# Feed-forward rounds with seven block products in place of eight, hidden tiles through memory, and the down product by thirds of the tokens

## What is computed

```python
h = _rmsnorm(x, lw["norm_ffn_w"]) * (1 + sc_f) + sh_f
ffn = (jax.nn.silu(h @ lw["ffn_w1"]) * (h @ lw["ffn_w3"])) @ lw["ffn_w2"]
x = x + g_f * ffn
```

## Time and profile before

| what | value |
| --- | --- |
| runs | 3107.42 us median of 3 (3106.93 to 3108.69) |
| span of the profiled execution | 3106.5 us |
| PE busy | 3060.1 us, 99% |
| PEld busy | 2941.0 us, 95% |
| DVE busy | 1539.3 us, 50% |
| ACT busy | 1217.6 us, 39% |
| POOL busy | 752.6 us, 24% |
| HBM | 210.90 MB read, 36.47 MB written |

### The profile page before, as it was taken

One profiled execution on the slowest core, in us unless ns is written; L12 is line 12 of the kernel. 1 busy time (PEld: TensorE's weight loads), 2 busy tenths in 40 slices (PEclk: granted clock), 3 DMA queues, 4 the chain that ended last, 5 costly groups with the idle time before them and its releaser, 6 DMA issues. The chain is left out here.

```text
span 3106.5 us, 59758 instructions
## 1 busy us (share of the span) xinstructions
PE 3060.1 (99%) x22180; PEld 2941.0 (95%) x22180; DVE 1539.3 (50%) x2647; ACT 1217.6 (39%) x2315; POOL 752.6 (24%) x936
## 2 busy tenths in 40 slices
PE   6999999999999999999999999999999999999998
PEld 5899999999999999999999999999999999999998
DVE  4646657568466574674656333444343222222233
ACT  6445455564554555545545442112241101210222
POOL 0024345245353462353534500000200000000002
PEclk9999999999999999999999999999999999999999
DMA  7622122122231221222212244434111111111112
GB/s 264 246 82 90 41 80 81 48 77 80 65 97 40 82 78 48 86 72 68 86 48 76 91 151 142 136 97 135 39 41 41 41 47 41 47 35 47 41 34 88
DMA packets 291362, 250.61 MB, mean 81 GB/s; under 512 B 10952, under 2 KB 262960, under 8 KB 291120
## 3 DMA queue, kind: packets, MB, share of 16 engines
q1 hardware_dynamic: 255552, 193.40, 20.3%
q10 hardware_dynamic: 35568, 54.02, 5.4%
HBM read 210.90 MB, written 36.47 MB: 80 GB/s over the span
## 5 line engine op out<-in xcount | busy, mean ns | idle before, releaser
L823 PE MATMUL bank<-h_hi,w_hi 128*128 128x384 f32 x2496 | 868.5, 348 | 2.5 <-ACT th L1416 2.5
L823 PE MATMUL bank<-h_hi,w_lo 128*128 128x384 f32 x2496 | 836.6, 335 | 0.0
L823 PE MATMUL bank<-h_lo,w_hi 128*128 128x384 f32 x2496 | 835.8, 335 | 0.0
L2147 PE MATMUL bank<-a_hi,v_hi 128*128 128x384 f32 x1440 | 483.1, 336 | 7.0 <-DVE v_lo L2367 2.5
L823 PEld LDWEIGHTS bank<-h_hi,w_hi 128*128 128x128 f32 x2496 | 469.4, 188 | 17.6 <-issue 7.3
L2147 PE MATMUL bank<-a_hi,v_lo 128*128 128x384 f32 x1440 | 481.1, 334 | 0.0
L2147 PE MATMUL bank<-a_lo,v_hi 128*128 128x384 f32 x1440 | 481.1, 334 | 0.0
L823 PEld LDWEIGHTS bank<-h_lo,w_hi 128*128 128x128 f32 x2496 | 469.8, 188 | 2.7
L823 PEld LDWEIGHTS bank<-h_hi,w_lo 128*128 128x128 f32 x2496 | 469.0, 188 | 0.0
L1935 POOL TENSOR_TENSOR kq<-kq,fg 128x384 f32<-128x384 f32 x288 | 290.0, 1036 | 176.3 <-PE bank L952 145.0
L2147 PE MATMUL bank<-b_hi,v_hi 128*128 128x384 f32 x912 | 306.3, 336 | 0.9 <-DVE v_lo L2367 0.9
(11 more groups left out here) (278 smaller groups left out, 4376.5 us busy)
## 6 DMA issues: line engine op xcount, KB each, us to landing
raw<-in_w_in SPq DMA_DIRECT2D x104, 512.0 KB, 4.1
cumb<-cum_scratch SPq DMA_DIRECT2D x72, 512.0 KB, 6.0
raw<-in_ffn_w SPq DMA_DIRECT2D x60, 512.0 KB, 3.8
ada_late<-in_ada_w SPq DMA_DIRECT2D x8, 2048.0 KB, 9.4
small<-gate_scratch ACTq DMA_DIRECT2D x72, 192.0 KB, 2.4
gate_scratch<-th ACTq DMA_DIRECT2D x48, 192.0 KB, 1.9
y_scratch<-x_t SPq DMA_DIRECT2D x8, 1152.0 KB, 4.8
small<-y_scratch ACTq DMA_DIRECT2D x48, 192.0 KB, 2.4
```

Source lines behind the costliest of these rows:

```text
L823: last = pe.matmul(out, w[i][:, k, :], h[:, k, blk(hb)], start=(k == 0 and j == 0), stop=(k == KT - 1 and j == 2))
L2147: last = pe.matmul(banks[3 * s + b][:, 0:BW], wp[s][:, k, :], operand[ap][:, k, blk(b)], start=(k == 0 and j == 0), stop=(k == kt - 1 and ...
```

## The change

One plain up round of the old kind makes hidden tile 0. The other 21 rounds are made by `pair`. There the two weight blocks of a round are seen as a 2 x 2 block matrix: x11, x12 are the low and high four k-tiles of w1 (`raw[0]`), x21, x22 those of w3 (`raw[1]`). The activations are 2 x 2 as well: low and high four k-tiles, first and second half of the tokens (576 each): a11, a12, a21, a22. Seven products of blocks and some sums give the four blocks of the result:

- sums of weights, in each round, on GpSimd (`s_sums_of`, L3089 to L3098): S1 = x21 + x22, S2 = S1 - x11, S3 = x11 - x21, S4 = x12 - S2. S1 and S3 share a buffer, S2 and S4 the other.
- sums of activations, once, on VectorE and GpSimd (`t_sum_of`, `t_fourth`, L3113), each 4 x 576 columns, split afterwards: T1 = a12 - a11, T2 = a22 - T1, T3 = a22 - a12, T4 = a21 - T2 (over a12).
- products o = 0 to 6: x11 a11, S2 T2, S1 T1, S3 T3, x12 a21, S4 a22, x22 T4, each as two parts j of 288 tokens with 4 k-tiles x 3 terms. Products 4, 5 and 6 add into the banks of 0, 2 and 3.
- sums of results: ScalarE copies product 0 away (`keep_p1`, L2504) before product 4 may add to its bank; VectorE adds U2 (L2837), C22 (L2843, L2845) before products 5 and 6 may add to their banks, C12 (L2855), C21 (L2865), and gates (L2850, L2860); ScalarE does the tanh (L2509, L2514); GpSimd multiplies (`hid_product`, L3107).

Each hidden tile (576 KB) is stored by SP to `hid_scratch`. The weights of the round after are loaded when all seven splits of the running round are made. The core of the diff:

```diff
+BLOCKS = 7
+STEPS = 2 * BLOCKS
+K_BLOCKS = (0, 4, 8, 12, 16, HID)
...
+            with sp.Fori(0, ROUNDS - 1) as rd:
+                sp.wait_ge(x_split, rd * BLOCKS + BLOCKS)
+                load_pair(rd + 1)
+                store_hid(rd)
...
+                        elif o == 4:
+                            pe.wait_ge(p1_kept, rd * 2 + (j + 1))
+                        elif o in (5, 6):
+                            pe.wait_ge(c22_done, rd * 2 + (j + 1))
+                        out = bank_of(o, j)[:, 0:SUB]
+                        for k, (hi, lo) in enumerate(moving(o, j)):
+                            for i, (wi, mv) in enumerate(((0, hi), (0, lo), (1, hi))):
+                                last = pe.matmul(out, w[wi][:, k, :], mv, start=(o < 4 and k == 0 and i == 0),
+                                                 stop=(k == KH - 1 and i == 2),
+                                                 skip_group_check=o >= 4)
+                        last.then_inc(prod_done, 1)
...
+            def pair(rd):
+                for j in range(2):
+                    keep_p1(rd, j, isinstance(rd, int) and rd == 0)
+                for o in range(4):
+                    x_high_part(rd + 1, o)
+                for j in range(2):
+                    tanh1(rd, j)
+                x_high_part(rd + 1, 4)
+                tanh2(rd, 0)
+                x_high_part(rd + 1, 5)
+                tanh2(rd, 1)
+                x_high_part(rd + 1, 6)
...
+                elif which == 3:
+                    pool.wait_ge(x_split, rd * BLOCKS + 3)
+                    pool.tensor_tensor(s0, x11, x21, ALU.subtract).then_inc(s_ready, 1)
```

```diff
+                hid_high_part(h)
...
+                act.activation(hid_hi[b][:, k, :], hid_in[h % 3], ACT.Copy).then_inc(hid_high, 1)
+                load_hid(h + 2)
...
+            def last_pair(rd):
+                for j in range(2):
+                    keep_p1(rd, j)
+                load_hid(0)
+                load_hid(1)
+                for h in range(8):
+                    hid_high_part(h)
+                tanh1(rd, 0)
+                d_high_part(0, 0)
...
+                    for k in range(K_BLOCKS[q], K_BLOCKS[q + 1]):
+                        if t == 0:
+                            pe.wait_ge(hid_split, HID * b + k + 1)
```

More of the change, by code:

```diff
@@ new lines, in down @@
+            def down(u):
+                b, t = divmod(u, OUTS)
+                if u >= 2:
+                    pe.wait_ge(d_added, u - 1)
+                else:
+                    pe.wait_ge(gate1_done, 2 * (ROUNDS - 1) + u + 1)
+                out = banks[u % 2][:, 0:BW]
+                for q in range(QS):
+                    pe.wait_ge(x_split, ROUNDS * BLOCKS + QS * u + q + 1)
+                    w = d_ring(q)
+                    for k in range(K_BLOCKS[q], K_BLOCKS[q + 1]):
+                        if t == 0:
+                            pe.wait_ge(hid_split, HID * b + k + 1)
+                        for i, (wi, mv) in enumerate(((0, hid_hi[b]), (0, hid_lo[b]), (1, hid_hi[b]))):
+                            last = pe.matmul(out, w[wi][:, k - K_BLOCKS[q], :], mv[:, k, :],
+                                             start=(k == 0 and i == 0), stop=(k == HID - 1 and i == 2))
+                    last.then_inc(d_multiplied, 1)
@@ L2203, in _ @@
                 elif name == "up0":
[L2204 to L2213 removed]
+                    for i in range(n):
+                        for s, b in TURNED:
+                            unit(name, i, s, b)
+                            if i == 0 and (s, b) == (0, 0):
+                                ones_product(2)
                 else:
@@ L2216, in _ @@
                         body(name, i)
+            pair(0, True)
+            with pe.Fori(1, ROUNDS) as rd:
+                pair(rd)
+            for u in range(NB * OUTS):
+                down(u)
+                b, t = divmod(u, OUTS)
+                if b > 0 and t == 0:
+                    add_squares(b - 1)
+                elif b > 0 and t == 1:
+                    turn_back(CB * b - 3)
+                    turn_back(CB * b - 2)
+                elif b > 0 and t == 2:
+                    turn_back(CB * b - 1)
+            turn_back(6)
+            turn_back(7)
+            add_squares(2)
+            turn_back(8)
         @block.scalar
@@ L2297, in body, with down @@
+            def down(u):
+                b, t = divmod(u, OUTS)
+                if u > 0:
+                    square_out(u - 1)
+                if b > 0 and t == 1:
+                    root(b - 1)
+                coming = hid_coming(b, t)
+                for q in range(QS):
+                    d_high_part(u + 1, q)
+                    if q < len(coming):
+                        hid_high_part(coming[q])
+            def body(name, i):
                 I = it(name, i)
@@ L2310, in body @@
                             act.dma_start(stage[b][:, :], dram_blk(y_dram, t + y0, b)).then_inc(small_in[b], 16)
-                        if b == 0 and not last_it and not (turned(name, i) and s == 0):
-                            high(s + 1, I, UNITS + 5 if turned(name, i) else None)
+                        if b == 0:
+                            high(s + 1, I)
                         if name in ("s1", "s2"):
@@ L2549, in _ @@
             pool.wait_ge(acc_done, acc_at("h", 3, 1, 2))
+            for late in cleared:
+                pool.sem_clear(late)
             for b in range(NB):
@@ L2580, in _, with s_sums_of @@
-            for b in range(NB):
-                add_square(KT - 2, b, (KT - 2) * NB + 2 * b)
+            def s_sums_of(rd, which):
+                x11, x12, x21, x22 = (raw[i][:, ks, :] for i in range(2) for ks in (slice(0, KH), slice(KH, KT)))
+                s0, s1 = (v[:, :].rearrange("p (k c) -> p k c", c=P) for v in s_sums)
+                if which == 1:
+                    for s in range(2):
+                        pool.wait_ge(x_raw[s], rd * 16 + 16)
+                    pool.tensor_tensor(s0, x21, x22, ALU.add).then_inc(s_ready, 1)
+                elif which == 2:
+                    pool.wait_ge(s_ready, rd * 4 + 1)
+                    pool.tensor_tensor(s1, s0, x11, ALU.subtract).then_inc(s_ready, 1)
+                elif which == 3:
+                    pool.wait_ge(x_split, rd * BLOCKS + 3)
+                    pool.tensor_tensor(s0, x11, x21, ALU.subtract).then_inc(s_ready, 1)
+                else:
+                    pool.wait_ge(s_ready, rd * 4 + 2)
+                    pool.tensor_tensor(s1, x12, s1, ALU.subtract).then_inc(s_ready, 1)
@@ new lines, in _ @@
+            pool.wait_ge(hi_done, PARTS["up"] + 24)
+            pool.wait_ge(parts, PARTS["up"] + 24)
+            second = slice(HALF, T)
+            pool.tensor_tensor(t_sum[:, T2], a_hi[:, KH:KT, second].bitcast(F32), a_lo[:, KH:KT, second].bitcast(F32),
+                               ALU.add).then_inc(h_summed, 1)
+            for which in (1, 2, 3, 4):
+                s_sums_of(0, which)
+            with pool.Fori(0, ROUNDS - 1) as rd:
+                for which in (1, 2, 3, 4):
+                    s_sums_of(rd + 1, which)
+                for j in (2, 3, 0, 1):
+                    hid_product(rd, j)
```

740 lines of the change are left out of this document (555 added, 185 removed).

## The result

| | before | after |
|---|---|---|
| median of the runs | 3108.06 us (3106.93 to 3110.67) | 3140.25 us (3136.76 to 3142.1) |
| ratio | | 1.0101, 95% interval 1.0087 to 1.0116 |
| span of the profiled execution | 3106.5 us | 3140.3 us |

The change makes the kernel 32 us slower, 1.0%; the forecast was 3133. So two measurements of one kernel can lie 4 to 5 us apart, and smaller differences between kernels are read here from their profiles and not from their times.

A forecast was written before the change was run, and what follows sets the result against it. TensorE, busy 99% of the span, was taken to bound the kernel before, a side chain the gated rounds after. Terms: -23 + 31.5 + 0.9 + 17 = +26 us, so 3107.4 + 26 = 3133 us, range 3098 to 3160.

The forecast's parts named there:

- Matmuls of 288 columns: Gated rounds on TensorE: 133 ns a matmul, 168 in 22.4 us, 2.5 us less in each of 21 rounds.
- the rival with 144 ns: Gated rounds: the weight load sets the pace, 24.2 us a round, 10 us more, 3143 us; chance 0.06.
- Side chain: Gated round: store, loads, sums, splits, gates and products take 23.7 us; TensorE needs 22.4 and waits 1.3 us a round.
- the ports' rival: Gated rounds: GpSimd and VectorE slow each other, chain about 1 us longer, 19 us more, 3152 us; chance 0.22.
- 23 us gained: Rounds 2 to 20: 19 x 23.7 = 450 us against 19 x 24.9 = 473.
- First gated round: Four TensorE waits, together 34 us on top of 22.4: 56.4 us against 24.9, 31.5 lost.
- GpSimd's 4.9 us sum hides under VectorE's first three: First gated round: GpSimd's activation sum of 4.9 us adds no time beside VectorE's three sums.
- The clock in that round: First gated round: lowered TensorE clock after gaps mostly falls into waits set by other engines; nothing added.
- Start of down: Down part's start: 14 hidden blocks ready, eight come at 1.3 us or wait for the last store; about 17 us waiting.
- Tail: Transposes, squares and stores at the end keep their length; the one new wait lies beside VectorE's work.
- the one with quicker transfers: Gated rounds: store and loads overlap, chain falls to 22.4 us, TensorE sets the round, 25 us less, 3108; chance 0.15.
- the faster one: Chain of 21.8 us, 130 ns a matmul, hidden blocks in 0.9 us each, down loses 6: 3086 us; chance 0.12.

The follow-up runs named there:

- the second time: The changed kernel with nothing further changed, timed again beside the follow-up runs: 3135.59 us (ratio 1.0089).
- the kernel with loads first: Changed kernel with SP issuing the weight loads of the round after next ahead of the gated blocks' store, not behind it: 3108.31 us.
- twice-stored: Changed kernel with one more store of 576 KB in front of each gated store: 3172.67 us (1.021).
- four kernels: Kernel combining four edits and a reordered first gated round, 3079.67 us; three variants reordering transfers at the start of down: 3079.27, 3077.56, 3076.62 us.

## Why the prediction was right, and where it was off

The sign, the mechanism and most of the size were right: +32 us measured and +28 the second time, +26 forecast, inside the range. Of the first profile's 33.8 us, 4.6 lie before the change, so 29 are the change's. Step by step:

- **Matmuls of 288 columns**: 133 ns forecast, 132 measured (200 us of the kernel with loads first). The load beside them sets nothing; the rival with 144 ns falls.
- **Side chain**: 23.7 us forecast, 23.75 measured, and the loads-first and twice-stored runs show it as the cause: 22.26 us without the store in front (there TensorE sets the round), 25.44 with two. Its terms, from the chain and the timelines of one round: store and loads 7.3 us (2619.92 to 2627.25), as forecast; GpSimd's two sums 2.7 (3.0). Two low parts beside GpSimd's sum and products took 1.03 and 1.24 us for 0.69, so the ports' rival was at work too, with 0.9 us a round, and about as much had been put too high elsewhere. It is no separate case: its price is in the 23.75.
- **"23 us gained" in rounds 2 to 20**, and 0.9 lost in the last: 22.1 together, 20.8 measured over the 20 rounds. The waits are 1.3 x 19 = 25 us as forecast and 25.8 as measured; that the sums agree so well is in part luck, since the 25.8 are 18 waits of 1.3 us in rounds 3 to 20 and one of 2.5 in the last.
- **First gated round**: 31.5 lost was forecast, 38.1 measured. This is the step that was off. "GpSimd's 4.9 us sum hides under VectorE's first three" is wrong: they take turns, the first product started 10.7 us late and not 6; with that sum on VectorE it is 6.3. The delay runs down VectorE's queue. Counted from the end of the plain round, the first, second, fifth and sixth products (each behind one of the four gaps) started at 10.7, 21.7, 41.8 and 55.2 us; the forecast's own steps give 6, 17, 35.6 and 49.3. So 4.7 us are there from the first product on. The further 1.5 us at the fifth are of the same kind: GpSimd's other two sums lie beside VectorE's low parts, of which one took 1.79 us for 0.69, and GpSimd's took 3.55 and 3.64. The last 1.5 us are the halved clock behind the last gap (48 matmuls in 7.8 us, 6.3 at full clock). So the round is 5.9 us late at the sixth product and 7.3 at its end; the forecast's sum stands 0.7 above its own steps, which leaves 6.6.
- **The clock in that round**: "here that mostly falls into waits that are set by the other engines, so I add nothing" was nearly right. In four stretches of 3.2, 6.0, 5.8 and 3.1 us, each behind one of the gaps, TensorE works at a granted clock of 0.5, its lower level of 1.2 GHz, where a matmul takes 0.24 us. Of the 63.0 us, 32.3 are gaps (10.8, 6.4, 8.0 and 7.7 from start to start, less a matmul each), 22.3 are matmuls at full clock, and 8.4 are left for the slower matmuls. But all but 1.5 of these 8.4 us took nothing from the time, since they only shortened the next gap: the chain of that round has no TensorE in it. It also shows from run to run: in four profiles of the same start (the changed kernel twice, the one with the hidden blocks on SP, the one with one more store) the four gaps sum to 33.0 to 34.1 us, while the sixth product starts 55.1 to 55.4 us behind the last plain matmul each time. The 1.5 us at the end were not priced, and round 2, which has no wait, takes most of them back: from the end of the first round's last wait to that of round 3 it is 47.9 us, two rounds of 23.95. No run changed the clock alone. That the four gaps together came out near the forecast's 34 is luck: the forecast had them at full clock and from an earlier start.
- **Start of down**: 17 us forecast, 13.0 measured. Right in kind, but eight blocks at 1.3 us are 10.4 us, the rest of the 17 has no working, and the count missed a cause: the third load of the first unit stood behind the last store, and ScalarE's blocks behind its high part (idle 6.28 us for it in the changed kernel, at 2842.76 us).
- **Tail**: no change forecast, and none: from the end of the last addition VectorE needs 7.1 us in both profiles.

The Trainium skill, page SBUF — State Buffer, section SBUF: two separate sides, has the shared port pair of VectorE and GpSimd as an exclusive lock. The trace agrees where both run long operations: VectorE's split of 1024 columns lasted until 1.1 us after GpSimd's sum, close to its own 1.2 us. The prediction's estimate by that rule was 2 us a round, as if the whole shorter operation were added each time; the rows show 0.9. They agree with turns all the same: the two low parts (2635.04 and 2639.01 us, 1.03 and 1.24 us long) began when GpSimd's operation beside each was under way, and both ended 0.55 us behind its end.

The rivals: the one with quicker transfers (3108) and the faster one (3086) fall with the chain's 23.75 us. One change of order in SP's queue makes TensorE set the round (22.26 us) and reaches 3108 by itself; no run had rounds shorter than that. The seven products in place of eight do pay when the side work is kept short of them: 3076.6 to 3079.7 us for four kernels, 0.9 to 1.0% faster than the kernel before.

## What to carry to other kernels

When the bounding engine gets less work, add up the cycle of all the others (each transfer with its place in the queue) before counting the gain; a store that a loop puts ahead of its next loads is part of that cycle, and swapping the two was worth 27 us here. The instruction that a wait names is not always the one to move: moving C22 closed its wait and left most of the period. A transition (operands to be formed, a new stage to be filled) costs what its longest chain costs, and work for it belongs under the last stretch of old work, not behind it. Do not add the halved clock behind each gap to the gaps: while another engine's chain ends the next wait, the slower matmuls come out of that wait, and only those behind the last gap are left to count (here 1.5 us of 8.4).

## What the runs showed of the hardware

- VectorE and GpSimd operations with both operands in SBUF take turns: VectorE's operation of 2304, 1024 or 512 columns ends 2.4, 1.1 or 0.55 us behind the end of the GpSimd operation that was under way. As lengths: 2304 columns 5.53 and 3.50 us beside GpSimd, 2.55 alone; 1024 columns 4.18 against 1.22; GpSimd's 512 columns 3.60 and 3.46 against 1.3.
- A matmul of 288 columns starts each 132 ns with a weight load of 128 rows beside it at full clock, 0.24 us at a granted clock of 0.5. A round whose pace another chain sets is as long at a granted clock of 0.93 as at 1.00 (25.47 and 25.46 us).
- A block of 192 KB landed in 2.31 us with no load of 512 KB from another queue in flight, and in 7.54 us with three.
- One more store of 576 KB ahead of two loads of 512 KB on one queue moves their landing from 5.7 to 6.9 us after the issue; behind them the same store leaves the round at TensorE's pace.
